# Up projection of the gated MLP: the last 64 gate and 64 value features share one tile of 128 stationary columns, and both last norm turns are issued together

## What is computed

```python
D_FF = 2752
CONV_WIDTH = 3

def conv_ffn(h, w_up, conv_w, conv_b, w_down):
    S = h.shape[1]
    u = h @ w_up
    up = jnp.pad(u, ((0, 0), (CONV_WIDTH - 1, 0), (0, 0)))
    c = conv_b + conv_w[0] * up[:, 0:S]
    for tap in range(1, CONV_WIDTH):
        c = c + conv_w[tap] * up[:, tap:tap + S]
    gate, val = jnp.split(c, 2, axis=-1)
    return (jax.nn.silu(gate) * val) @ w_down
```

## Time and profile before

| | |
|---|---|
| median of 3 runs | 1343.82 us (1342.89 to 1344.29) |
| span of the profiled execution | 1344.7 us; this is all that the page gives of its time |
| PE busy | 1314.8 us, 98% |
| PE weight loads busy | 883.8 us, 66% |
| DVE busy | 884.6 us, 66% |
| ACT busy | 365.6 us, 27% |
| POOL busy | 270.1 us, 20% |
| HBM | 88 GB/s over the span |

### The profile page before, as it was taken

One profiled execution on the slowest core, in us unless ns is written; L12 is line 12 of the kernel. 1 busy time (PEld: TensorE's weight loads), 2 busy tenths in 40 slices (PEclk: granted clock), 3 DMA queues, 4 the chain that ended last, 5 costly groups with the idle time before them and its releaser, 6 DMA issues.

```text
span 1344.7 us, 16228 instructions
## 1 busy us (share of the span) xinstructions
PE 1314.8 (98%) x5728; PEld 883.8 (66%) x5728; DVE 884.6 (66%) x2049; ACT 365.6 (27%) x900; POOL 270.1 (20%) x264
## 2 busy tenths in 40 slices
PE   4999999999999999999999999999999999999998
PEld 3544455544544545886455556888788888888887
DVE  5888999679431555564455676676676777777564
ACT  4223121225200102223455676110133233330000
POOL 1168578215003387700000000001000000000000
PEclk9899999999999999999999999999999999999999
DMA  9773524651312112302102002112212313224210
GB/s 320 180 153 100 157 42 143 198 184 36 121 38 77 63 63 63 125 32 94 63 1 64 1 1 61 66 63 89 84 63 82 107 63 125 64 68 167 77 58 32
DMA packets 89996, 120.59 MB, mean 90 GB/s; under 512 B 15448, under 2 KB 51614, under 8 KB 89916
## 3 DMA queue, kind: packets, MB, share of 16 engines
q1 hardware_dynamic: 85216, 110.81, 26.6%
q10 hardware_dynamic: 2956, 5.05, 1.2%
q0 software_dynamic: 1744, 3.70, 1.0%
HBM read 111.00 MB, written 6.84 MB: 88 GB/s over the span
## 4 chain that ended last, share of the span: by engine, by line
PE 94%; DVE 3%; ACT 1%; issue 1%; DMA 1%; ACTq 0%; POOL 0%; DVEq 0%; POOLq 0%
PE bank L1502 18%; PE bank L872 12%; PE bank L1528 10%; PE bank L885 9%; PE bank L1429 7%; PE bank L1387 6%; PE bank L907 5%; PE bank L1160 4%; PE bank L1270 4%; PE bank L1341 3%; PE bank L1367 3%; PE bank L936 2%; PE bank L1472 2%; PE bank L1205 2%; PE bank L1043 1%
## 5 line engine op out<-in xcount | busy, mean ns | idle before, releaser
L1502 PE MATMUL bank<-arena 128*128 128x256 f32 x1120 | 242.0, 379 | 0.0
L1502 PEld LDWEIGHTS bank<-arena 128*128 128x128 f32 x1120 | 212.7, 190 | 29.3 <-issue 0.4
L872 PE MATMUL bank<-arena 128*128 128x512 f32 (+1 forms) x384 | 157.0, 565 | 0.0
L1528 PE MATMUL bank<-arena 128*128 128x256 f32 x616 | 133.1, 379 | 0.0
L885 PE MATMUL bank<-arena 128*128 128x512 f32 x288 | 127.7, 596 | 0.0
L1528 PEld LDWEIGHTS bank<-arena 128*128 128x128 f32 x616 | 117.0, 190 | 15.9
L907 PEld LDWEIGHTS bank<-arena 128*128 128x128 f32 (+2 forms) x660 | 78.4, 144 | 72.3 <-issue 41.9
L872 PEld LDWEIGHTS bank<-arena 128*128 128x128 f32 x384 | 71.9, 190 | 77.8 <-issue 73.6
L907 PE MATMUL bank<-arena 128*128 128x128 f32 (+2 forms) x660 | 94.0, 280 | 20.4 <-ACT arena L1612 7.1
L2913 DVE CUSTOM_DVE_ANT_0 arena<-bank,arena 128x128 f32<-128x128 f32 (+3 forms) x128 | 57.8, 489 | 73.1 <-PE bank L1341 72.3
L1429 PE MATMUL bank<-arena 128*128 128x256 f32 x448 | 97.6, 379 | 0.0
(11 more groups left out here) (387 smaller groups left out, 1951.6 us busy)
## 6 DMA issues: line engine op xcount, KB each, us to landing
arena<-in_w_in SPq DMA_DIRECT2D x14, 2048.0 KB, 7.8
arena<-in_w_up SPq DMA_DIRECT2D x20, 1024.0 KB, 6.6
arena<-in_w_ada SPq DMA_DIRECT2D x16, 512.0 KB, 8.9
arena<-in_w_down SPq DMA_DIRECT2D x8, 1024.0 KB, 7.3
arena<-in_w_out SPq DMA_DIRECT2D x2, 2048.0 KB, 9.3
arena<-in_w_attn_br SPq DMA_DIRECT2D x8, 512.0 KB, 7.3
arena<-in_w_o SPq DMA_DIRECT2D x2, 2048.0 KB, 7.6
rb_dram<-rb_one_dram ACTq DMA_DIRECT2D x1, 2560.0 KB
```

Source lines behind the costliest of these rows:

```text
L872: mm = pe.matmul(ps[:, 0:n], act[:, k, 128 * t:128 * t + 128], w[:, k, 0:n], start=(k == 0), stop=(k == kt - 1))
L1502: mm = pe.matmul(ps, left[:, k, :], right[:, k, :], start=(first and k == 0), stop=(k == 3), skip_group_check=True)
L1528: mm = pe.matmul(down_acc(i, name), left, right, start=first and name in ("P1", "P7", "P2", "P4"), stop=last, skip_group_check=True)
```

## The change

The 64 gate and 64 value features of tile 21 become one stationary tile of 128 columns, named `fgv`, in one bank (2): the gate on partitions 0 to 63, the value on 64 to 127. For this their weights are loaded side by side in the slot (columns 128 to 191 gate, 192 to 255 value), in three DMAs instead of two, and the value's convolution weights of that tile go to partitions 64 to 127. ACT reads the two halves of the bank in two bias operations, and DVE applies the first added tap to the value on partitions 64 to 127. The second added tap reads there and writes to partitions 0 to 63, after a copy of the two columns that this tap doesn't reach, so that gate and value can be multiplied. Turns 2 and 3 now stand together, ahead of `fgv`; before, turn 2 stood ahead of and turn 3 behind the first half of tile 21's gate.

```diff
-        for n, j in enumerate(UP_ORDER[:2]):
-            proj_at(("fg", j), 2 * n)
-            proj_at(("fv", j), 2 * n + 1)
+        for n, name in enumerate((("fg", FT - 2), ("fv", FT - 2), ("fgv", FT - 1))):
+            proj_at(name, n)
...
-        for J in (FT // 2 - 1, *range(FT // 2 - 1)):
-            n = 256 if J < FT // 2 - 1 else 192
-            chunk(("f", J), ("proj", ("fv", FT - 1)) if J == FT // 2 - 1 else ("product", 14 * J + 14), KT, 512,
-                  [(0, n, lambda J=J, n=n: cols_of(w_up_2, 0, KT, 256 * J, 256 * J + n)),
-                   (256, 256 + n, lambda J=J, n=n: cols_of(w_up_2, 0, KT, DFF + 256 * J, DFF + 256 * J + n))])
+        F0 = 256 * (FT // 2 - 1)
+        chunk(("f", FT // 2 - 1), ("proj", ("fgv", FT - 1)), KT, 512,
+              [(0, 192, lambda: cols_of(w_up_2, 0, KT, F0, F0 + 192)),
+               (192, 256, lambda: cols_of(w_up_2, 0, KT, DFF + F0 + 128, DFF + F0 + 192)),
+               (256, 384, lambda: cols_of(w_up_2, 0, KT, DFF + F0, DFF + F0 + 128))])
...
-            for j in (FT - 2, FT - 1):
-                for a, key in enumerate(("fg", "fv")):
-                    begin_proj((key, j))
-                    up_part(a, key, j, slice(0, 256))
-                    if a != j - (FT - 2):
-                        row_turn("h3", xn3, 3 - a, (xn_done, 2 * TT + 4 - a))
+            for name, c0 in UP_FIRST:
+                if name == ("fgv", FT - 1):
+                    for t in range(2, TT):
+                        row_turn("h3", xn3, t, (xn_done, 2 * TT + t + 1))
+                begin_proj(name)
+                up_part(name, c0, slice(0, 256))
             for t in range(2, TT):
                 for a in range(2):
                     aux_out(pe, ("h3", t, a))
-            for j in (FT - 2, FT - 1):
-                for a, key in enumerate(("fg", "fv")):
-                    up_part(a, key, j, slice(256, 512)).then_inc(proj_done, 1)
+            for name, c0 in UP_FIRST:
+                up_part(name, c0, slice(256, 512)).then_inc(proj_done, 1)
...
+            proj_ready(act, ("fgv", FT - 1))
+            for a in range(2):
+                rows = slice(64 * a, 64 * a + 64)
+                up_bias(a, FT - 1, pbank(("fgv", FT - 1))[rows, :], rows)
+            up_tanh(FT - 1, 64)
...
-                    pool.dma_start(cvr[r0 + FT - 1:r0 + FT, a, 0:64], src[128 * (FT - 1):DFF].rearrange("(j p) -> j p", p=64))\
+                    pool.dma_start(cvr[r0 + FT - 1:r0 + FT, a, 64 * a:64 * a + 64], src[128 * (FT - 1):DFF].rearrange("(j p) -> j p", p=64))\
...
-                f_ = fc[0:m, n % 2, a, :]
-                step(v.scalar_tensor_tensor(f_[:, 1:S], src[:, 0:S - 1], cvw[0:m, a, 1, j:j + 1], f_[:, 1:S],
+                f_ = fc[rows, n % 2, a, :]
+                to = f_ if rows.start == 0 else fc[0:64, n % 2, a, :]
+                step(v.scalar_tensor_tensor(f_[:, 1:S], src[:, 0:S - 1], cvw[rows, a, 1, j:j + 1], f_[:, 1:S],
                                             ALU.mult, ALU.add))
-                step(v.scalar_tensor_tensor(f_[:, 2:S], src[:, 0:S - 2], cvw[0:m, a, 0, j:j + 1], f_[:, 2:S],
+                if rows.start:
+                    v.tensor_copy(to[:, 0:2], f_[:, 0:2])
+                step(v.scalar_tensor_tensor(to[:, 2:S], src[:, 0:S - 2], cvw[rows, a, 0, j:j + 1], f_[:, 2:S],
                                             ALU.mult, ALU.add))
...
+            for a in range(2):
+                rows = slice(64 * a, 64 * a + 64)
+                up_taps(a, FT - 1, pbank(("fgv", FT - 1))[rows, :], rows)
+            v.sem_inc(pfree(("fgv", FT - 1)), 1)
+            up_act(FT - 1, 64)
```

More of the change, by code:

```diff
@@ L487, in program @@
         wchunk("wo1", ("s", 7, "P4"), w_o_2, KT, 512)
-        for J in (FT // 2 - 1, *range(FT // 2 - 1)):
-            n = 256 if J < FT // 2 - 1 else 192
-            chunk(("f", J), ("proj", ("fv", FT - 1)) if J == FT // 2 - 1 else ("product", 14 * J + 14), KT, 512,
-                  [(0, n, lambda J=J, n=n: cols_of(w_up_2, 0, KT, 256 * J, 256 * J + n)),
-                   (256, 256 + n, lambda J=J, n=n: cols_of(w_up_2, 0, KT, DFF + 256 * J, DFF + 256 * J + n))])
+        F0 = 256 * (FT // 2 - 1)
[3 more added lines that the diff above has]
+               (256, 384, lambda: cols_of(w_up_2, 0, KT, DFF + F0, DFF + F0 + 128))])
+        for J in range(FT // 2 - 1):
+            chunk(("f", J), ("product", 14 * J + 14), KT, 512,
+                  [(256 * a, 256 * a + 256, lambda J=J, a=a: cols_of(w_up_2, 0, KT, DFF * a + 256 * J, DFF * a + 256 * J + 256))
+                   for a in range(2)])
         for a in range(2):
@@ L1463, in _, with up_part @@
             s_products(7, "P3", "P4")
[L1465 to L1470, removed]
+            UP_FIRST = [(("fg", FT - 2), 0), (("fv", FT - 2), 256), (("fgv", FT - 1), 128)]
+            def up_part(name, c0, cols):
+                w = weights(pe, ("f", FT // 2 - 1))
                 for k in range(KT):
-                    mm = pe.matmul(ps[0:m, cols], w[:, k, c0:c0 + m], hT[:, k, cols], start=(k == 0), stop=(k == KT - 1))
+                    mm = pe.matmul(pbank(name)[:, cols], w[:, k, c0:c0 + 128], hT[:, k, cols], start=(k == 0), stop=(k == KT - 1))
                 return mm
@@ L1994, in _, with up_bias @@
             s_copies(7, 0, 4)
-            def up_bias(a, j, src):
-                m = src.shape[0]
+            def up_bias(a, j, src, rows=slice(0, 128)):
                 n = UP_AT[j]
@@ L2001, in up_bias @@
                     act.wait_ge(act_done, n - 1)
-                act.activation(fc[0:m, n % 2, a, :], src, ACT.Identity,
-                               scale=cvw[0:m, a, 2, j:j + 1], bias=cvw[0:m, a, 3, j:j + 1]).then_inc(tap_done, 1)
+                act.activation(fc[rows, n % 2, a, :], src, ACT.Identity,
+                               scale=cvw[rows, a, 2, j:j + 1], bias=cvw[rows, a, 3, j:j + 1]).then_inc(tap_done, 1)
             def up_tanh(j, m=128):
@@ L2018, in _ @@
             act.wait_ge(cvw_done, 2)
[L2019 to L2023, removed]
+            for a, key in enumerate(("fg", "fv")):
+                proj_ready(act, (key, FT - 2))
+                up_bias(a, FT - 2, pbank((key, FT - 2))[:, :])
+            up_tanh(FT - 2)
+            proj_ready(act, ("fgv", FT - 1))
[3 more added lines that the diff above has]
+            up_tanh(FT - 1, 64)
             for J in range(NG // 2 + 1):
@@ L3144, in up_blocks, with up_taps @@
                 v.tensor_tensor(upS[:, a, 1, 0:256], u2, p74, ALU.add).then_inc(block_done, 1)
-            def up_taps(a, j, src, m=128):
+            def up_taps(a, j, src, rows=slice(0, 128)):
                 n = UP_AT[j]
                 v.wait_ge(tap_done, TAP[a, j] + 1)
-                f_ = fc[0:m, n % 2, a, :]
-                step(v.scalar_tensor_tensor(f_[:, 1:S], src[:, 0:S - 1], cvw[0:m, a, 1, j:j + 1], f_[:, 1:S],
+                f_ = fc[rows, n % 2, a, :]
+                to = f_ if rows.start == 0 else fc[0:64, n % 2, a, :]
+                step(v.scalar_tensor_tensor(f_[:, 1:S], src[:, 0:S - 1], cvw[rows, a, 1, j:j + 1], f_[:, 1:S],
                                             ALU.mult, ALU.add))
-                step(v.scalar_tensor_tensor(f_[:, 2:S], src[:, 0:S - 2], cvw[0:m, a, 0, j:j + 1], f_[:, 2:S],
+                if rows.start:
+                    v.tensor_copy(to[:, 0:2], f_[:, 0:2])
+                step(v.scalar_tensor_tensor(to[:, 2:S], src[:, 0:S - 2], cvw[rows, a, 0, j:j + 1], f_[:, 2:S],
                                             ALU.mult, ALU.add))
@@ L3219, in _ @@
             weight_sums(0)
[L3220 to L3224, removed]
+            for a, key in enumerate(("fg", "fv")):
+                up_taps(a, FT - 2, pbank((key, FT - 2))[:, :])
+                v.sem_inc(pfree((key, FT - 2)), 1)
+            up_act(FT - 2)
+            for a in range(2):
[3 more added lines that the diff above has]
+            up_act(FT - 1, 64)
             for J in range(NG // 2 + 1):
```

## The result

| | before | with the change |
|---|---|---|
| median | 1344.05 us (1342.89 to 1346.74, 4 runs) | 1335.73 us (1334.8 to 1336.88, 4 runs) |
| ratio | | 0.9943, 95% interval 0.993 to 0.9955 |
| first up matmul to first product of the up groups | 30.25 us | 22.47 us |
| first up matmul to the last instruction | 409.0 us | 401.1 us |

The forecast was 1336.0 us and a stage of 22.48 us. The kernel became faster by 0.57% of its time, and both numbers of the forecast hold. The ratio is the one on record; the quotient of the two medians is 0.9938, inside the interval.

The account below looks back on a forecast made before the run. PE (TensorE), busy 98% of the span, was taken as the bound. Fewer matmuls (6.91 us) and removed seams (0.86) sum to 7.77 us off 1343.82, giving 1336.0 us; all else cost 0. Range 1334.8 to 1338.2 us.

Parts of the forecast that it names:

- PE bounds, and what leaves the stage leaves the program: PE busy 98% of the span; shortening the stage (first up matmul to up groups) moves the end equally.
- 64 matmuls become 48: Up tiles on PE: 128 records become 96 at 0.216 us each, saving 6.91 us.
- The seams: Six places in the stage where shape 128x64 begins or ends: removing them saves 0 to 0.86 us, 0.86 taken.
- Rival A: Pauses at the shape changes stay, so only 6.91 us is saved: 1336.9 us, chance 0.10.
- Turns together, no wait: Turns 2 and 3 adjacent on PE: cost 0, DVE's copies ready 1.9 us before PE needs them.
- DVE keeps up: DVE's group 1 weight sums end 8.4 us into the next stage, PE wants them at 13.8: room 5.4, cost 0.
- B: ACT's copy or DVE's sums miss PE's group 0 deadline: PE waits 1 to 2 us, 1337 to 1338, chance 0.10.
- C: DVE's half-to-half operations so slow that PE loses more than it saved: 1348.6 us at 18 us excess, chance 0.01.
- ACT keeps up: ACT's first product copy ends 3.7 us into the next stage, PE needs it at 6.9: room 3.2, cost 0.
- Loads hidden: First tiles' weights in three DMAs: at most 2.9 us for 256 B pieces, hidden under 17 us before PE's use.
- The sentence that narrow matmuls run one behind the other at the full price: Tile 21's 64-column matmuls on PE: 0.224 us a record, no cheaper than full width, no overlap.
- The trace disagrees: Against the skill's parallel tiles, by which stacking saves next to nothing: gate and value write the same 64 partitions without overlap.

Follow-up runs that it names:

- experiment 3: The kernel before, with tile 21's 64 matmuls kept but taking 128 stationary columns throughout: stage 29.38 us, ratio to before 0.9988.
- 1: The kernel before with only turns 2 and 3 put together ahead of tile 21, no stacked tile: stage 29.96 us, ratio to before 0.9998.
- experiment 4: The changed kernel with the stacked tile done as two narrow tiles, alternating between the halves of the bank: stage 23.06 us, ratio to before 0.995.
- experiment 2: The changed kernel with turn 3 put back behind the stacked tile's first half: stage 23.88 us, ratio to before 0.9945.
- experiments 5 to 7: The changed kernel with 3, 8 and 6 DVE operations added ahead of group 1's weight sums: ratios to before 0.9949, 0.9993 and 0.9981.
- experiments 6 and 7: The changed kernel with 8 and 6 added DVE operations: 408.5 and 405.3 us to the end, ratios to before 0.9993 and 0.9981.
- Experiment 6: The changed kernel with eight added DVE operations (10.03 us): 408.5 us to the end, ratio to before 0.9993.
- The control: The changed kernel measured again as it is, beside the other runs: stage 22.46 us, ratio to before 0.9944.

## Why the prediction was right, point by point

- **PE bounds, and what leaves the stage leaves the program**: shown. 371.00 of 371.00 us busy behind the stage, and the stretch from the first product of the up groups to the end is 378.7 us before (1344.7 - 965.96) and after (1334.3 - 955.65).
- **64 matmuls become 48, 6.91 us**: experiment 3 against the changed kernel, two kernels with one shape throughout, differs by 29.38 - 22.47 = 6.91 us.
- **The seams, 0.86 us, taken in full**: shown by experiment 3 (0.87) and, in other numbers of them, by 1 and 4. Rival A (they stay) is wrong.
- **Turns together, no wait**: no idle time in front of the turns or behind them. The copies end 10.0 us after the stage's start (943.21), forecast 10.2, and PE wants them at 12.1. The forecast gave this move a cost of 0 and no gain; experiment 2 puts its worth at 1.4 us, as a wait that the stacked tile alone would have made. The forecast didn't price what happens without it.
- **DVE keeps up**: its sums for group 1 end at 964.16, 8.5 us after the next stage's start, forecast 8.4. The room of 5.4 us was found to be 5.3 by experiments 5 to 7. The half-to-half operations cost 0.17 and 0.75 us, forecast 0.15 and 0.74, so neither B nor C had a mechanism.
- **ACT keeps up**: the first copy ends 3.65 us after the start (958.92 + 0.38, one of the two in that row), forecast 3.7. Its room of 3.2 us was not tested.
- **Loads hidden**: at 916 to 918 us the rate is 0 already in the changed kernel, with PE's first use at 933.18:

```profile
916.00:918.00 2.00, 2.00 (x11) 1.77 (x10) 1.20 (x4) 0.38 (x1) 0.00 (x0) 1.00 0.00 0
```

- **What was priced wrongly in a rival**: C counted a wait of PE at its own length. Had DVE been late by more than its room, the loss would have been larger than the wait, as experiments 6 and 7 show: C's point of break-even, 13.2 us of lateness, would have been nearer to 10.5 (room 5.3, then a saving of 7.8 less 2.6 us of clock; worked out, not run). Experiment 6 is close to it: 10.0 us of lateness leave 0.5 us of the saving to the end (409.0 against 408.5).
- **The sentence that narrow matmuls run one behind the other at the full price** holds for these two tiles as they were issued. The reason given there, the same 64 partitions, fits experiment 4, which doesn't separate it from the order. "The trace disagrees" was too strong as well: two tiles on the same partitions can't speak against what is said there of different tiles, and experiment 4, with different ones, agrees with it. As a statement on narrow matmuls it is wrong: the attention part of the same trace has 16 narrow records (L1367) within 1.95 us, and experiment 4 repeats that here. It changes nothing in the sum, since the kernel before did pay for both tiles; alternating halves would have saved the same 6.91 us.
- **How close the time came** is in part luck. The range took its width from three runs, whose ends around 1336.0 give 1335.1 to 1336.5 us and not the "some 1335.0 to 1336.8" written, and it knew nothing of the start-up's draws. The control's six runs of the same kernel lie between 1333.88 and 1338.64 us, outside the range at both ends. The stage, 22.47 us against 22.48, is what bears out the mechanism.

Nothing here beats the changed kernel. One idea was not tried: tile 20's gate and value as one more seven-product group in place of eight products, four matmuls or 1.7 us less on PE by the same rows, with sums that DVE would have to make in time.

## What to carry to other kernels

Where PE never idles, count its matmuls by their moving columns: two stationary tiles of 64 columns that share the moving operand belong in one of 128, or should at least be issued alternately on different halves of the output partitions. Then look at what the removed matmuls had covered: here a turn had to move ahead, or 1.4 us of the 7.8 would have come back as a wait. Before calling an engine's lateness harmless, measure its room, and price a wait of PE above its own length.

## What the runs showed that was not expected

- Entering or leaving the 128x64 shape costs PE 0.14 to 0.15 us on average in this f32 stream: six places 0.87 us, four 0.57 to 0.59.
- A pause of PE of 2.23 us was followed by the 1.2 GHz level and 1.9 us of loss, one of 4.75 us by 2.6 us of loss. One of 1.18 us was followed by none.
- PE's clock in the start-up differs from run to run. In ten profiles of nine kernels with the same start-up on PE, the stage starts at 930.8 to 931.1 us with no stretch at 1.2 GHz (six profiles), at 933.2 with one (two) and at 935.0 and 935.7 with two.
- A DVE operation that reads partitions 64 to 127 and writes 0 to 63 takes 0.75 us for 64x510, as one that stays on its partitions does.
